# A fused two-layer recurrent trunk: the mLSTM sample tile is taken second, and GpSimd's masks ahead of its decays

## The reference

```python
def _layer(x, st, w):
    x = _layer_norm(ALPHA * x + 0.5 * _swiglu(x, ...), ...)
    p = x @ w['w_in']
    ya, shift, wkv = _rwkv7(p[..., :RWKV_COLS], ...)         # 8 heads of 64, matrix state
    yb, conv, C, n, m = _mlstm(p[..., RWKV_COLS:], ...)      # 4 heads of 128, matrix memory C
    mix = jnp.concatenate([ya, yb], axis=-1) @ w['w_out']
    ...
# in _mlstm, for each chunk
s = jnp.einsum('bhtd,bhsd->bhts', qc, kc) * jnp.exp(dmat - m_t[..., None])
num = g_inter[..., None] * jnp.einsum('bhtd,bhde->bhte', qc, C) + jnp.einsum('bhts,bhse->bhte', s, vc)
den = g_inter * jnp.einsum('bhtd,bhd->bht', qc, n) + s.sum(-1)
h = num / jnp.maximum(jnp.abs(den), jnp.exp(-m_t))[..., None]
C = dec[..., None, None] * C + jnp.einsum('bhs,bhsd,bhse->bhde', ws, kc, vc)
# behind the chunks: mean and variance of h per head, h normalised, times sigmoid(o_pre)
```

## Time and profile before

| what | value |
|---|---|
| median of 3 runs (lowest to highest) | 1522.2 us (1518.78 to 1522.57) |
| profiled execution: time, span | 1519.59 us, 1517.9 us |
| PE busy | 1464.3 us (96%) |
| DVE busy | 985.0 us (65%) |
| ACT, POOL busy | 695.9 us (46%), 378.2 us (25%) |
| chain that ended last, by engine | PE 85%, DVE 7%, ACT 3%, issue 2% |
| busy in 400 to 450 us: PE, DVE, ACT, POOL | 44.06, 31.82, 23.66, 20.18 us |

### The profile page before, as it was taken

How to read it: one execution, slowest core, us unless ns; L and a number is a source line. 1 busy time by engine, 2 the same in 40 slices (tenths; PEclk the granted TensorE clock), 3 DMA queues, 4 the chain that set the end, 5 groups by cost and what they waited for, 6 DMA issues and landing times.

```text
span 1517.9 us, 33992 instructions
## 1 busy us (share of the span) xinstructions
PE 1464.3 (96%) x13374; PEld 1409.3 (93%) x13374; DVE 985.0 (65%) x1579; ACT 695.9 (46%) x1188; POOL 378.2 (25%) x407
## 2 busy tenths in 40 slices
PE   7999999999989999999999999989999899999995
PEld 7999998899867999999999999979998689999995
DVE  4444435588476687775577776466865777877644
ACT  5333334765645543334443334366565465333332
POOL 4222363010532422220412222300115323222100
PEclk9999999999999999999999999999999999999998
DMA  8544543443214555444544545434521444555351
GB/s 221 150 144 149 168 149 88 126 128 101 55 34 134 157 160 151 146 141 150 159 137 142 151 152 156 152 88 123 129 78 33 123 121 136 165 150 167 126 166 35
DMA packets 318938, 198.82 MB, mean 131 GB/s; under 512 B 7792, under 2 KB 303760, under 8 KB 318832
## 3 DMA queue, kind: packets, MB, share of 16 engines
q1 hardware_dynamic: 315120, 190.69, 43.1%
q0 software_dynamic: 3712, 6.62, 2.1%
HBM read 188.50 MB, written 8.78 MB: 130 GB/s over the span
## 4 chain that ended last, share of the span: by engine, by line
PE 85%; DVE 7%; ACT 3%; issue 2%; DVEq 1%; DMA 0%; POOL 0%; SPq 0%; POOLq 0%; ACTq 0%
PE bank L2120 24%; PE bank L2122 23%; PE bank L2121 23%; DVE wlo L2613 2%; PE bank L2207 1%; DVE rlo L2644 1%; ACT whi L2410 1%; ACT z L1183 1%; PE bank L2212 1%; PE bank L764 1%; PE bank L752 1%; DVE raw L1578 1%; PE bank L2171 1%; PE bank L853 1%; PE bank L458 1%
## 5 line engine op out<-in xcount | busy, mean ns | idle before, releaser
L2410 ACT ACTIVATE whi<-raw 128x1024 fp32r<-128x1024 f32 x340 | 358.2, 1059 | 471.9 <-PE bank L2122 455.7
L2613 DVE TENSOR_TENSOR wlo<-raw,whi 128x1024 fp32r<-128x1024 f32 x340 | 421.2, 1243 | 230.1 <-ACT whi L2410 229.3
L2120 PE MATMUL bank<-rhi,whi 128*128 128x322 f32 x984 | 306.5, 311 | 0.0
L2122 PE MATMUL bank<-rhi,wlo 128*128 128x322 f32 x984 | 305.9, 311 | 0.0
L2121 PE MATMUL bank<-rlo,whi 128*128 128x322 f32 x984 | 304.8, 310 | 0.0
L2120 PE MATMUL bank<-xh,whi 128*128 128x320 f32 x912 | 286.2, 314 | 4.6 <-DVE xl L2787 3.5
L2121 PE MATMUL bank<-xl,whi 128*128 128x320 f32 x912 | 283.0, 310 | 0.0
L2122 PE MATMUL bank<-xh,wlo 128*128 128x320 f32 x912 | 282.9, 310 | 0.0
L2882 POOL TENSOR_TENSOR hl<-scratch,hh 128x320 f32 x88 | 146.9, 1669 | 495.4 <-DVE scratch L2734 379.7
L2120 PE MATMUL bank<-hh,whi 128*128 128x320 f32 (+1 forms) x704 | 218.4, 310 | 0.5 <-DVE wlo L2613 0.5
L2121 PE MATMUL bank<-hl,whi 128*128 128x320 f32 (+1 forms) x704 | 217.4, 309 | 0.0
(11 more groups left out here) (421 smaller groups left out, 1888.8 us busy)
## 6 DMA issues: line engine op xcount, KB each, us to landing
raw<-in_ffn_wg SPq DMA_DIRECT2D x88, 512.0 KB, 3.8
raw<-in_ffn_wu SPq DMA_DIRECT2D x88, 512.0 KB, 3.8
raw<-in_ffn_wd SPq DMA_DIRECT2D x88, 512.0 KB, 3.6
raw<-in_w_in SPq DMA_DIRECT2D x60, 512.0 KB, 3.8
raw<-in_w_out SPq DMA_DIRECT2D x16, 512.0 KB, 6.1
raw<-in_state_C SPq DMA_DIRECT2D x8, 512.0 KB, 6.1
out_s_C<-raw SPq DMA_DIRECT2D x8, 512.0 KB, 4.1
ring<-in_state_wkv POOLq DMA_DIRECT2D x8, 256.0 KB, 5.5
```

What stands on the lines that cost most here:

```text
L2120: pe.matmul(out, w_hi, hi, start=start, stop=False)
L2122: return pe.matmul(out, w_lo, hi, start=False, stop=stop)
L2410: act.activation(whi[:, slot, :], raw[:, slot, :], ACT.Copy).then_inc(hi_ready.sem, 1)
L2613: dve.tensor_tensor(wlo[:, slot, :], raw[:, slot, :], whi[:, slot, :].bitcast(F32), ALU.subtract).then_inc(lo_ready.sem, 1)
```

## The change

The order of the mLSTM tiles becomes prompt 0, samples, prompt 1 (`TURN` gives a tile's place). The sample heads are normalised first (`g = 1`), the prompt's behind them. Of the eight memory pieces six now come in steps 14 to 16, ahead of the prompt scores in step 17, which wait for them since both use banks 4 to 6, and two in step 22. The samples get their own `rexp_s`, as their factors are now needed longer. On POOL the first masked values come ahead of the zeroing, the second behind the sample heads, and the decays behind them; the first memory term waits for the prompt means instead of the first spreads.

```diff
+        rexp_s = area(5656, HB * TS, of=ring)
...
-        vmask = [area(1536, SB, DK, of=spare), area(15304, SB, DK)]
+        vmask = [area(9480, SB, DK), area(15304, SB, DK)]
...
-                pe.wait_ge(num_ready.sem, num_ready.by(L, n))
-                pe.wait_ge(caug_ready.sem, caug_ready.by(L, n))
+                pe.wait_ge(num_ready.sem, num_ready.by(L, TURN[n]))
+                pe.wait_ge(caug_ready.sem, caug_ready.by(L, 1))
+                if n == 1:
+                    pe.wait_ge(left_done.sem, left_done.by(L, FIRST_LEFT))
...
+        TURN = (0, 2, 1)
...
-        LEFT = (("C", 0), ("C", 1), ("C", 2), ("C", 3), ("H", 0), ("H", 1), ("C", 4), ("C", 5), ("C", 6), ("C", 7),
-                ("H", 2), ("N", 0), ("T", 0))
+        LEFT = (*(("C", i) for i in range(2 * HB)), ("H", 2), ("H", 0), ("H", 1), ("N", 0), ("T", 0))
+        FIRST_LEFT = 6
...
-        NUM_AT = (7, 12)
-        SCORES_AT = (9, 14)
-        HEAD_AT = (17, 18)
-        LEFT_AT = (20, 20, 21, 21, 22, 22, 23, 23, 24, 24, 25, 26, NSTEP)
+        NUM_AT = (7, 20)
+        SCORES_AT = (9, 17)
+        HEAD_AT = (12, 13)
+        LEFT_AT = (14, 14, 15, 15, 16, 16, 22, 22, 23, 25, 25, 26, NSTEP)
...
-        SQUARES_AT = (17, 20)
-        ROOTS_AT = (19, 22)
+        SQUARES_AT = (18, 21)
+        ROOTS_AT = (20, 23)
...
-        ADDED_AT = (8, 13)
-        QUERIES_AT = 17
-        INTER_AT = 17
-        MEANS_AT = (17, 20)
-        SPREADS_AT = (19, 21)
-        SCALED_AT = (20, 23)
+        ADDED_AT = (8, 21)
+        QUERIES_AT = 12
+        INTER_AT = 13
+        MEANS_AT = (18, 21)
+        SPREADS_AT = (20, 23)
+        SCALED_AT = (21, 24)
...
             pool.wait_ge(kv_ready.sem, kv_ready.by(L, 2 * NTT))
+            masked_values(pool, L, 0)
             pool.memset(qm[:, :, :], 0.0).then_inc(qm_zero.sem, 1)
...
-            pool.wait_ge(hvar_ready.sem, hvar_ready.by(L, 1))
+            pool.wait_ge(num_mm.sem, num_mm.by(L, NTT))
+            pool.wait_ge(hmean_ready.sem, hmean_ready.by(L, 2))
             memory_term(pool, L, 1)
-            pool.wait_ge(left_mm.sem, left_mm.by(L, 10))
+            pool.wait_ge(left_mm.sem, left_mm.by(L, 2 * HB))
             memory_term(pool, L, 3)
```

More of the change, by code:

```diff
@@ L666, in hymba_kernel @@
         NSIDE = MEMS + SB // 2
-        SIDE_AT = [*range(KEYS), 9, 10, 11, 13, 14, 15, 16, 17, 19, 20, 21, 23, 24]
+        SIDE_AT = [*range(KEYS), 9, 10, 11, 13, 14, 15, 16, 17, 19, 21, 22, 23, 24]
         assert len(SIDE_AT) == NSIDE
@@ L1112, in tile_weights @@
             rows = TT[n][1]
-            act.wait_ge(tile_mm.sem, tile_mm.by(L, n + 1))
+            act.wait_ge(tile_mm.sem, tile_mm.by(L, TURN[n] + 1))
             if n:
-                act.activation(rexp[:, 0:HB * rows], bank[5][:, 0:HB * rows], ACT.Exp)
-            act.wait_ge(wlog_ready.sem, wlog_ready.by(L, n + 1))
+                act.activation((rexp if n == 1 else rexp_s)[:, 0:HB * rows], bank[5][:, 0:HB * rows], ACT.Exp)
+            act.wait_ge(wlog_ready.sem, wlog_ready.by(L, TURN[n] + 1))
             act.activation(wexp[0:rows, :, 0:rows], wexp[0:rows, :, 0:rows], ACT.Exp).then_inc(wexp_ready.sem, 1)
@@ L1473, in own_queries @@
             own = qm[:, h, :].rearrange("p (b s) -> p b s", b=SB)[:, :, 0:ST]
-            dve.tensor_tensor(own, seqs(qk[:, h, TP:T]), seqs(rexp[:, h * TS:(h + 1) * TS]),
+            dve.tensor_tensor(own, seqs(qk[:, h, TP:T]), seqs(rexp_s[:, h * TS:(h + 1) * TS]),
                               ALU.mult).then_inc(qm_ready.sem, 1)
@@ L1479, in tile_products @@
             at, rows, _ = tile_views(n)
-            dve.wait_ge(wexp_ready.sem, wexp_ready.by(L, n + 1))
+            dve.wait_ge(wexp_ready.sem, wexp_ready.by(L, TURN[n] + 1))
             if n:
                 dve.tensor_tensor(qh[:, :, 0:rows], qk[:, 0:HB, at:at + rows],
-                                  rexp[:, 0:HB * rows].rearrange("p (h t) -> p h t", h=HB), ALU.mult)
+                                  (rexp if n == 1 else rexp_s)[:, 0:HB * rows].rearrange("p (h t) -> p h t", h=HB),
+                                  ALU.mult)
             dve.scalar_tensor_tensor(
@@ L1527, in head_means @@
             tt, stt, ts = dve.tensor_tensor, dve.scalar_tensor_tensor, dve.tensor_scalar
-            dve.wait_ge(num_ready.sem, num_ready.by(L, 2 + g))
+            dve.wait_ge(num_ready.sem, num_ready.by(L, NTT - g))
             if g:
+                dve.drain()
                 tt(num[0:TS, 2, :, DK], num[0:TS, 2, :, DK], inter[0:TS, 32:36], ALU.add)
@@ L1577, in left_over_done @@
                     at = h * TS + s * ST + ST - 1
-                    last = dve.scalar_tensor_tensor(out=C0[:, h, s, :], in0=C0[:, h, s, :], scalar=rexp[:, at:at + 1],
+                    last = dve.scalar_tensor_tensor(out=C0[:, h, s, :], in0=C0[:, h, s, :], scalar=rexp_s[:, at:at + 1],
                                                     in1=b[:, k * DK:(k + 1) * DK], op0=ALU.mult, op1=ALU.add)
@@ L1581, in left_over_done @@
                 at, rows = TT[i]
-                if i == 0:
+                if i == 2:
                     dve.wait_ge(og_ready.sem, og_ready.by(L, 1))
```

69 lines of the change are left out of this document (36 added, 33 removed).

## The result

The changed kernel takes 1533.39 us (median of 5, 1525.17 to 1535.85) against 1522.20 before (5 runs, 1518.78 to 1523.99): 1.0065 times, interval 1.0042 to 1.0088. That is slower, and above the forecast's range. The profiled execution was the fastest of the five, 1525.17 us, which is the sum worked out for it (1525.2). The other four lie at 1532 to 1536. So two things are to be explained: whether the sum was right for the right reasons, and what the other executions have on top.

What follows compares the result with a forecast made beforehand. Mixers bound by PE and ACT, then mostly DVE; 0.2 us plus collisions of 2.6 per layer, 5.6 in two, gave 1525.2 on the profiled execution and 1527.8 on the median; forecast 1526 us, range 1515 to 1531.

Steps and rivals of the forecast that it cites:

- the sum worked out for it: Whole kernel: 0.2 us and collisions of 2.6 in each of two layers, 5.6 on the profiled 1519.6, giving 1525.2.
- the anchors: Mixers of the old trace: PE begins second-tile scores at 407.85, third-tile scores at 421.48; recurrence at 459.59, 51.74 us behind the first.
- the walk: First layer's new order in three stretches, sample scores to recurrence: without collisions the recurrence begins at 459.8, 0.2 us later.
- the first stretch: Sample scores to prompt scores: 5.7, 7.3 and 8.8 us, so the prompt scores' wait for the sixth memory piece ends at 429.7.
- POOL's collisions: In the tail, POOL's memory terms shut out DVE's scalings: +2.6 us per layer, bounds 0 and 4.1.
- The first: Sample scaling beside POOL's first memory term: ends 2.8 us behind the prompt means, not 1.16, +1.65 per layer.
- The second: Prompt scaling beside POOL's third memory term, which waits for the prompt spreads: about +0.95 us per layer.
- The clock rival: Tail, PE waiting for DVE: lower clock adds 3 us in two layers on top of collisions, 1528.2 us; 15%.
- its sign of 2: In the tail: the two turned prompt outputs taking over 2 us would show that the clock fell.

Runs made afterwards that it cites:

- loads_apart: Changed kernel with each of POOL's four state loads issued only when the one ahead has landed: 1523.68 us, 1.0012 times the kernel before.
- mem1_behind: Changed kernel with POOL's first memory term waiting for the sample scaling instead of the prompt means: 1534.34 us, 1.0066 times the kernel before.
- after_again: The changed kernel once more with no edit, profiled and timed five times: 1530.87 us, 1.0057 times the kernel before.
- before_apart: The kernel before with POOL's four state loads issued one behind another's landing: 1522.11 us, 0.9995 times the kernel before.
- before_wout_apart: The kernel before with SP's loads of the output weights issued one at a time: 1518.04 us, 0.9971 times the kernel before.
- scale_early: Changed kernel with spreads, roots and scaling of the sample heads one step earlier each: 1530.12 us, 1.0058 times the kernel before.
- fill_four: Changed kernel with four unread matmuls on PE in its wait behind the prompt means: 1538.66 us, 1.0106 times the kernel before.
- both_apart: Changed kernel with state loads and output-weight loads each issued one at a time: 1525.28 us, 1.0010 times the kernel before.

## Why the prediction was wrong

**What bounds, the anchors, the walk.** Behind the prompt scores the walk held within 0.2 us in the first layer, and the gaps of DVE at scores, values and copies were 1.80, 2.05 and 1.33, near those walked (1.5, 2, 1).

**The step that failed** is the first stretch: "the four state loads in its queue come that much later; both are still ahead of their users". The step asked who uses the loads' data, and took the sample heads' times from a place in the old program where no loads were under way. What was missing is PE's code: it comes behind the queued loads, which cost 7 to 10 us of the median by loads_apart. In the changed kernel's two profiles that is seen as a stop of 1.0 to 2.8 us in each layer. With the loads apart the changed kernel is at 1.0012 (0.9998 to 1.0026).

**POOL's collisions** were right as a mechanism and too dear in the sum. The first is there to the tenth (2.76 behind the means, 2.8 worked out) and goes when the term is moved (1.25). The second, put at 0.95, cost 0.25 in the first layer and nothing in the second, since DVE first stood 0.77 and 0.97 for ACT's root, which took the place of that loss in the tail. By the rule that the prediction cites from the Trainium skill (SBUF — State Buffer, Who interferes with whom) a shut-out lasts for the whole instruction, and the traces agree again: 1.45 beside a memory term and 0.68 without one, 1.80 and 1.17. But the time at DVE didn't come out at the end: mem1_behind has it back and is not faster, in executions with a lower mean clock (0.977 against 0.9815).

**The recurrence** was taken as unchanged. It became 1.27 and 0.85 shorter, most likely because the earlier outputs, of which the prediction said that nothing waits for them, draw the weight loads out of the way of PE's code. So the profiled execution's sum was right by luck, by misses that cancel: 1.8 and 2.0 more in the first stretch (stops of 1.00 and 1.46 among them) against 2.1 from the recurrence and 1.55 from an earlier start of the mixers.

**The clock rival** got 15% and 1.5 us a layer in the tail. A low stretch is in both profiles of the changed kernel and in those of all its variants, mostly longer: at the lower level for 6.8 us in each layer of the first profile, 13.6 (3.4 of it behind the stop) and 10.2 in after_again, against 3.4 in the kernel before's. It lay elsewhere than the rival had it: the two prompt outputs took 1.06 (L458 in the chain above), under its sign of 2, and the sample output ahead of them 1.90. Nor is it the changed order's alone: before_apart and before_wout_apart, variants of the kernel before, have 3.4 and 17.1. Over executions, the time goes with the mean granted clock: 0.75 us for each 0.001 in 28 executions of the kernel before (mean 0.9839) and 1.1 in 11 of the changed one (mean 0.9815). Read off these two lines at a clock of 0.983, the kernels stand at 1523.3 and 1530.1, so some 7 us of the mean difference of 9.1 are there at equal clock, and 2 are clock. On the same footing loads_apart is at 1524.3, so 5.8 of what it gives back are there at equal clock, and before_wout_apart at 1521.1, so only some 2 of its 4.4. This is a fit, and in after_again the clock falls behind a stop for code as well, so the two parts aren't cleanly separate.

What stays open is what brings the clock down in the tail. Less waiting of PE in one place did not keep it up (scale_early, fill_four), and where its low stretch reaches into the recurrence it costs most (27 to 29 us to the output product without, 31 to 34 with 10 us or more of it). Why the changed order has a lower mean clock than the old one wasn't settled.

## What to carry to other kernels

Ahead of moving a block of many short matmuls, look at which large transfers are queued at its new place, and not only at who reads them: a stop that the chain calls "issue", with an instruction packet among the transfers, is the sign. Issue such loads one behind another's landing where their users can wait; here that was worth 7 to 10 us in the changed kernel (state loads) and 4 in the kernel before (output weights), clock included. And a sum over one profiled execution is the sum for that execution's clock: look at the clocks of the others before it is put on the median.

## What the runs showed of the hardware

PE's instructions arrive in packets of 16 KB on a queue of their own (queue 8) during the execution: in all 30 stops PE went on 1.26 to 1.66 us behind such a packet's end. With 1 MB of loads queued PE stopped up to 2.83 us in after_again; with one load of 256 KB in flight, not at all in loads_apart, and up to 1.00 at the same matmuls in both_apart. The Trainium skill (DMA: Bandwidth & Descriptors, Queues, rings and completion order) says that a DMA engine takes packets in turn from the queues that have work. By that the code should pass a long queue of one other kind with little delay; the runs show that the number of loads queued at once matters (stops of 3.3 us an execution in the mean with four, 0.6 with one), and no view of these traces shows where in between the code waited.
